# A gated decoder layer in split fp32 on one core: four plain gate-up jobs at the head of the feed-forward part, two half-width jobs in its middle

## The chip, the cores and the metric

The kernel runs on one core of a Trainium2 chip. TensorE (PE) multiplies matrices into PSUM; VectorE (DVE), ScalarE (ACT) and GpSimd (POOL) read and write SBUF and work beside it; SyncE (SP) issues most of the transfers. The metric is the device time of one execution in microseconds (us), the median of several.

## The reference

One layer of a decoder with 1024 channels, for 1024 prompt tokens and 8 sample tokens (1032 in all). The first part (attention, spatial gating, output projection, a residual) is not touched, except at its very end. The second part is what matters here:

```
h = _rmsnorm(x, g_fp)
f = (jax.nn.silu(h @ w_g) * (h @ w_u)) @ w_d
x = x + _rmsnorm(f, g_fq)
```

`w_g` and `w_u` are 1024 x 2816, `w_d` is 2816 x 1024.

## The kernel before

**Numbers.** Every fp32 operand of a product is held as two parts: a high part (ACT copies the operand into fp32r) and a low part (DVE subtracts the high part from the operand). A product is three matmuls: high by high, high by low, low by high.

**Shapes.** The 1032 tokens are four quarters of 258 columns (`NQ`); two quarters make a half (h = 0 or 1). The 2816 hidden channels are 22 tiles of 128 (`NF`). A *job* j multiplies one tile of `w_gate` and one of `w_up` by one half or by both. PE's order is the order of the program: the last units of the output projection (`wo_tile`, 24 units), then the 26 jobs, then the down projection `down(n, c)`, 16 times two.

**Blocks.** A job is seven *blocks* (`STEP`) for each half. A block is four steps in k times three matmuls, 12 matmuls of 128x258. With seven in place of eight, a job forms the 2 x 2 block product (Winograd's form of Strassen's method): it needs sums of the weight blocks (four per tile pair: POOL, `sums_in` three and `last_sum` one) and sums of the activation blocks (S1 to S4, four per half: three `f_sum` on POOL, one `f_third` on DVE), and it reads intermediate products back from PSUM (ACT copies one of them to `p1`; DVE makes seven sums and products in `ev`, `u2`, `u3`, C22, C21, prod1, C12, prod0, lines 2398 to 2456). Several blocks can start only when such a sum is there: the product is added up over the block's result in PSUM and SBUF in turn.

**Half jobs.** `HALVES` gives half 0 alone to jobs 0 to 3 (`AHEAD = 4`: half 1 isn't there yet), both halves to jobs 4 to 21, and half 1 alone to jobs 22 to 25, which load the weights of tiles 0 to 3 again. A job with both halves takes turns: a block of half 0, the same block of half 1. Each half has a set of three PSUM banks; in a job with one half the set is `j % 2`.

**Splits.** The weight blocks go through six slots (`SLOTS`). `high(q)` on ACT waits until the block six earlier has been used by PE, `low(q)` on DVE follows it (line 2324), and block q waits for `low(q)`. The activation blocks are split once: `f_high` on ACT (line 1687), `f_low` on DVE for A11, A12, S2, S1 (line 2318) and on POOL for S3, A22, S4 (line 2627). Their source is filled by `f_copy` (DVE) from PE's transposes (`f_turn`), the last three of which stand in job 2.

**Queues.** SP's queue is in program order: `job_load(j)` (1 MB of weights into one of two buffers, behind a wait for the splits of job j - 2), then `store(j - 2)`, which puts the result into HBM. At j = 23 twelve loads (`a_load(0)`, `a_load(1)`, the results of two quarters for the down projection) stand ahead of `store(21)` and `job_load(24)`. In `down` of n = 8, `z_first_sums` stands between the two halves and waits for POOL.

Of the kernel before, what the change touches and what calls it, by code (L numbers as in the profile page):

```python
# [12 lines left out]
ALU = mybir.AluOpType  # L13
# [66 lines left out]
F_HIGH = (0, 2, 1, 3, 4, 5, 6)  # L80
F_LOW = {0: (0, 1), 2: (0, 2), 1: (0, 3), 4: (0, 4), 3: (1, 1), 5: (1, 2), 6: (1, 3)}
# [4 lines left out]
DOWN = 7 * NJ  # L86
SPLITS = DOWN + 6 * 16
EVENTS = 7 * PAIRS
# [5 lines left out]
def tile_of(j):  # L94
    return j if j < NF else j - NF


def number(j, what, h, of):
    return len(of) * BEFORE[j] + of.index(what) * len(HALVES[j]) + HALVES[j].index(h) + 1


def event(j, o, h):
    return 7 * BEFORE[j] + o * len(HALVES[j]) + HALVES[j].index(h) + 1


def summed(j, what, h):
    return number(j, what, h, SUMS)


def silued(j, what, h):  # L110
    return number(j, what, h, SILUS)
# [7 lines left out]
def earlier(j, h):  # L119

    for i in range(j - 1, -1, -1):
        for g in reversed(HALVES[i]):
            if set_of(i, g) == set_of(j, h):
                return i, g
# [7 lines left out]
def used_after(q):  # L132

    if q < DOWN:
        return event(q // 7, q % 7, HALVES[q // 7][-1])
    return down_event((q - DOWN) // 6, 1, (q - DOWN) % 6)

# [42 lines left out]
def build(nc, A, O):  # L180
# [19 lines left out]
    with ctx:  # L200
# [105 lines left out]
        s0 = {i: at(f"s0_{i}", [P, 4, NQ], F32, R[3] + 4128 * i)[0] for i in (0, 1, 5)}  # L306
# [92 lines left out]
        f_tok, f_t, f_c, f_d = sem("f_scaled"), sem("f_turned"), sem("f_copied"), sem("f_s3_or_dec_done")  # L399
# [3 lines left out]
        sa_s, fh_s, fl_d, fl_p = sem("f_sums"), sem("f_hi"), sem("f_lo_dve"), sem("f_lo_pool")  # L403
# [4 lines left out]
        a_out, a_in = [sem(f"a_stored{i}") for i in range(2)], [sem(f"a_landed{i}") for i in range(6)]  # L408
        ah_s, al_s = sem("a_hi"), sem("a_lo")
# [23 lines left out]
        def f_raw(h, o):  # L433

            if STEP[o] in ("A11", "A12", "S3", "A22"):
                k = 4 * (STEP[o] in ("A12", "A22"))
                return fb[:, q_at(2 * h + (STEP[o] in ("S3", "A22"))), k:k + 4, :]
            return (s1 if h else s0)[{"S1": 0, "S2": 1, "S4": 5}[STEP[o]]][:, :, :]

        def f_lo(h, o):  # L440

            if STEP[o] in ("A11", "A12", "S3", "A22"):
                k = 4 * (STEP[o] in ("A12", "A22"))
                return fb_lo[:, q_at(2 * h + (STEP[o] in ("S3", "A22"))), k:k + 4, :]
            return (f1 if h else f0)[{"S1": 0, "S2": 1, "S4": 5}[STEP[o]]][:, :, :]

        def f_hi(h, o):
            return (f1 if h else f0)[{"A11": 2, "S2": 3, "A12": 4, "S3": 6, "S1": 7, "A22": 8, "S4": 9}[STEP[o]]][:, :, :]
# [29 lines left out]
        def split_source(q):  # L478
            if q < DOWN:
                w = w_pair(q // 7)  # L480
                return (w[:, 0, 0:4], tw[:, 1, :].rearrange("p (k c) -> p k c", k=4), w[:, 0, 4:8],
                        tw[:, 0, :].rearrange("p (k c) -> p k c", k=4), w[:, 1, 0:4], w[:, 0, 0:4], w[:, 1, 4:8])[q % 7]
# [40 lines left out]
        def _(sp):  # L523
# [92 lines left out]
            def job_load(j):  # L616

                if j >= 2:
                    sp.wait_ge(sp_lo, 7 * (j - 1))
                for e, w in enumerate((wg, wu)):  # L620
                    sp.dma_start(w_pair(j)[:, e], chunks(w, 0, 8, P * tile_of(j), P)).then_inc(raw_in[j % 2], 16)

            def store(j):
                hs = HALVES[j]
                cols = slice(2 * NQ * hs[0], 2 * NQ * hs[0] + 2 * NQ * len(hs))
                sp.wait_ge(sum_s, summed(j, "prod0", hs[-1]))
                sp.dma_start(a_d[tile_of(j)][:, cols], ab_of(j)[:, cols]).then_inc(a_out[j % 2], 16)

            def a_load(q):
                for kg, (k, n) in enumerate(KG):  # L630
# [2072 lines left out]
```

## Time and the profile before

| what | value |
|---|---|
| median of 3 runs | 1564.37 us (1560.65 to 1566.7) |
| the profiled execution's own time | 1565.85 us |
| its span in the trace | 1564.1 us |
| PE busy | 1491.3 us, 95% of the span |
| DVE, ACT, POOL busy | 757.0, 603.5, 270.0 us |
| mean granted TensorE clock | 0.981 |

The span is the trace from its first to its last instruction; the time has 1.75 us more around it. A matmul's busy time includes what the next one overlaps, so the spacing of matmuls is read from their starts, and PE's loss from its idle time and its granted clock (1.0 is 2.4 GHz).

### The profile page before, as it was taken

To read this page: it belongs to the slowest core of one execution; us is meant where nothing else is said; L and a number is where in the kernel's file an instruction comes from. 1 tells how busy PE (TensorE), PEld (TensorE's weight loads), DVE (VectorE), ACT (ScalarE), POOL (GpSimd) and SP (SyncE) were. 2 spreads that over 40 slices of the span, in tenths; PEclk is the share of its full clock that TensorE was granted. 3 is DMA by queue.
4 is the path that set the end of the run, shared out by engine and by line. 5 is a ranking of instruction groups with operands and counts; after the bars stand their busy time and mean duration, and the time that the engine had idled before them with its cause. 6 is when DMAs were issued, how large, how long until landed. Compare 5 with 4: busy or idle time off the path is not lost.

```text
span 1564.1 us, 26636 instructions
## 1 busy us (share of the span) xinstructions
PE 1491.3 (95%) x10953; PEld 1441.7 (92%) x10953; DVE 757.0 (48%) x1347; ACT 603.5 (39%) x1198; POOL 270.0 (17%) x253
## 2 busy tenths in 40 slices
PE   7999999999999999999876999999999689999998
PEld 6999999999999999987666999999999689999998
DVE  6105551343124464836789555666666473225322
ACT  6225543452224412446664333333333253335321
POOL 2000000000000132600545322222222120002000
PEclk9999999999999999999979999999999889999999
DMA  5111112001112153245532222222222746346341
GB/s 190 54 40 41 41 55 85 28 28 41 41 36 78 59 148 105 69 162 200 151 108 68 68 82 82 82 82 82 82 82 77 217 107 185 85 115 190 116 142 55
DMA packets 186665, 147.09 MB, mean 94 GB/s; under 512 B 7002, under 2 KB 168802, under 8 KB 186548
## 3 DMA queue, kind: packets, MB, share of 16 engines
q1 hardware_dynamic: 182656, 133.31, 28.3%
q0 software_dynamic: 2720, 7.89, 1.7%
q10 hardware_dynamic: 1172, 4.23, 0.7%
q8 instruction: 85, 1.39, 0.4%
q14 instruction: 32, 0.26, 0.1%
HBM read 121.84 MB, written 23.58 MB: 93 GB/s over the span
## 4 chain that ended last, share of the span: by engine, by line
PE 82%; DVE 6%; issue 3%; POOL 3%; ACT 2%; DMA 2%; SPq 1%; DVEq 0%; ACTq 0%; POOLq 0%
PE bank L734 8%; PE bank L736 8%; PE bank L735 8%; PE bank L1275 5%; PE bank L1276 5%; PE bank L1277 5%; PE psAB L1205 3%; PE bankC L734 3%; PE bank L1205 3%; PE bankC L736 3%; PE psAB L1207 3%; PE psAB L1206 3%; PE bankC L735 3%; PE bank L1206 3%; PE bank L1207 3%
## 5 line engine op out<-in xcount | busy, mean ns | idle before, releaser
L734 PE MATMUL bank<-h_hi,w_hi 128*128 128x344 f32 x752 | 247.9, 330 | 2.7 <-ACT g_pre L1345 2.2
L736 PE MATMUL bank<-h_hi,w_lo 128*128 128x344 f32 x752 | 240.1, 319 | 0.0
L735 PE MATMUL bank<-h_lo,w_hi 128*128 128x344 f32 x752 | 239.9, 319 | 0.0
L1275 PE MATMUL bank<-a_hi,s_hi 128*128 128x258 f32 x704 | 201.3, 286 | 0.0
L1276 PE MATMUL bank<-a_lo,s_hi 128*128 128x258 f32 x704 | 199.8, 284 | 0.0
L1277 PE MATMUL bank<-a_hi,s_lo 128*128 128x258 f32 x704 | 199.8, 284 | 0.0
L1884 DVE TENSOR_TENSOR w_lo<-w_raw,w_hi 128x1024 fp32r<-128x1024 f32 x71 | 90.8, 1279 | 202.0 <-ACT w_hi L1315 140.1
L1205 PE MATMUL psAB<-f,s_hi 128*128 128x258 f32 x440 | 128.9, 293 | 33.7 <-DVE ev L2411 13.9
L734 PEld LDWEIGHTS bank<-h_hi,w_hi 128*128 128x128 f32 x752 | 141.4, 188 | 7.4 <-issue 6.1
L735 PEld LDWEIGHTS bank<-h_lo,w_hi 128*128 128x128 f32 x752 | 141.3, 188 | 0.0
L736 PEld LDWEIGHTS bank<-h_hi,w_lo 128*128 128x128 f32 x752 | 141.3, 188 | 0.0
L1205 PE MATMUL bank<-f,s_hi 128*128 128x258 f32 x440 | 127.3, 289 | 11.3 <-ACT ev L1782 7.2
L1276 PEld LDWEIGHTS bank<-a_lo,s_hi 128*128 128x128 f32 x704 | 134.8, 191 | 0.0
L1275 PEld LDWEIGHTS bank<-a_hi,s_hi 128*128 128x128 f32 x704 | 134.2, 191 | 0.1
L1277 PEld LDWEIGHTS bank<-a_hi,s_lo 128*128 128x128 f32 x704 | 134.1, 190 | 0.0
L1708 ACT ACTIVATE s_hi<-raw 128x512 fp32r<-128x512 f32 x130 | 80.6, 627 | 127.5 <-PE psAB L1207 101.7
L1207 PE MATMUL psAB<-f,s_lo 128*128 128x258 f32 x440 | 127.1, 289 | 0.0
L1207 PE MATMUL bank<-f,s_lo 128*128 128x258 f32 x440 | 126.5, 287 | 0.0
L1205 PEld LDWEIGHTS psAB<-f,s_hi 128*128 128x128 f32 x440 | 86.2, 196 | 35.4 <-DVE ev L2411 14.1
L2324 DVE TENSOR_TENSOR s_lo<-rawd,s_hi 128x512 fp32r<-128x512 f32 x96 | 60.7, 646 | 115.1 <-ACT s_hi L1708 115.0
L2324 DVE TENSOR_TENSOR s_lo<-raw,s_hi 128x512 fp32r<-128x512 f32 x130 | 96.2, 771 | 21.7 <-ACT s_hi L1708 21.7
L1205 PE MATMUL bankC<-f,s_hi 128*128 128x258 f32 x352 | 100.4, 285 | 2.7 <-DVE ev L2424 2.0
(497 smaller groups left out, 3640.6 us busy)
## 6 DMA issues: line engine op xcount, KB each, us to landing
rawd<-in_w_down SPq DMA_DIRECT2D x32, 704.0 KB, 6.5
w_raw<-in_w_in SPq DMA_DIRECT2D x42, 512.0 KB, 4.0
raw<-in_w_gate SPq DMA_DIRECT2D x26, 512.0 KB, 4.0
raw<-in_w_up SPq DMA_DIRECT2D x26, 512.0 KB, 5.3
w_raw<-in_w_out SPq DMA_DIRECT2D x24, 512.0 KB, 3.7
a_raw<-a_rows SPq DMA_DIRECT2D x20, 516.0 KB, 7.3
a_rows<-ab SPq DMA_DIRECT2D x18, 516.0 KB, 2.7
xin<-in_x_prompt SPq DMA_DIRECT2D x8, 512.0 KB, 7.7
```

Source lines behind the costliest of these rows:

```text
L734: mm(out[:, 0:TG], w_hi[par][:, ws], hi[:, k, tgc[tg]], start=first, stop=False)
L735: mm(out[:, 0:TG], w_hi[par][:, ws], lo[:, k, tgc[tg]], start=False, stop=False)
L736: return mm(out[:, 0:TG], w_lo[par][:, ws], hi[:, k, tgc[tg]], start=False, stop=last)
L1205: mm(out, hi[:, k, :], xh[:, k, :], start=(begin and k == 0), stop=False, skip_group_check=True)
L1206: mm(out, hi[:, k, :], xl[:, k, :], start=False, stop=False, skip_group_check=True)
L1207: ins = mm(out, lo[:, k, :], xh[:, k, :], start=False, stop=(k == 3), skip_group_check=True)
L1275: mm(out, hi[:, k, :], xh[:, k, :], start=(kg == 0 and k == 0), stop=False)
L1276: mm(out, hi[:, k, :], xl[:, k, :], start=False, stop=False)
L1277: ins = mm(out, lo[:, k, :], xh[:, k, :], start=False, stop=(k0 + k == NF - 1))
L1708: fn(slot(q, 0), split_source(q), ACT.Copy).then_inc(sp_hi, 1)
L1884: v.tensor_tensor(w_lo[par][:], w_raw[par][:], w_hi[par][:].bitcast(F32), ALU.subtract).then_inc(w_lo_s, 1)
L2324: v.tensor_tensor(slot(q, 1), split_source(q), slot(q, 0).bitcast(F32), ALU.subtract).then_inc(sp_lo, 1)
```

## The change

Jobs 0 to 3 form all eight plain block products of half 0: `plain(j, o)` on PE has four weight blocks (B11, B21, B12, B22), each multiplied with two quarters. The gate product goes to banks 0 and 1 (c = 0, 1), the up product to banks 2 and 3 or 4 and 5. It is read back in two steps: ACT takes the gate bank through SiLU, DVE multiplies that with the up bank. No weight sums and no activation sums are needed for it. The sums of the activations (S1 to S4) and all low parts of activations move from POOL to DVE and stand later, in jobs 1 to 4; POOL makes the weight sums of jobs 4 to 25 alone. The half-1 jobs are now 9, 16, 24 and 25 (`ALONE`). The loads of the second quarter are spread: groups 2 to 5 follow the stores of their tiles, groups 0 and 1 and the first quarter come around job 25; `down_load(0)` comes earlier. `z_first_sums` stands three groups into `down(8, 1)`. The splits of the first quarter's results, two a job in jobs 23 to 25, now stand at the end of job 25 (two) and in `down(0)` (four). The diff, cut to its core:

```diff
+ALONE = (9, 16, 24, 25)
 NJ = NF + AHEAD
-HALVES = [(0,)] * AHEAD + [(0, 1)] * (NF - AHEAD) + [(1,)] * AHEAD
-BEFORE = [sum(len(x) for x in HALVES[:j]) for j in range(NJ + 1)]
-PAIRS = BEFORE[NJ]
+HALVES = [(0,) if j < AHEAD else (1,) if j in ALONE else (0, 1) for j in range(NJ)]
+TILE = [ALONE.index(j) if j in ALONE else j - sum(a < j for a in ALONE) for j in range(NJ)]
+PLAIN = ("B11", "B21", "B12", "B22")
...
+FIRST = [4 * min(j, AHEAD) + 7 * max(j - AHEAD, 0) for j in range(NJ + 1)]
+DOWN = FIRST[NJ]
...
+            done = [max(j for j in range(NJ) if 0 in HALVES[j] and TILE[j] < k + n) for k, n in KG]
+                if j > 12:
+                    for kg in range(2, 6):
+                        if done[kg] == j - 3:
+                            stored(j - 2)
+                            a_load(1, kg)
+                if j == NJ - 2:
+                    down_load(0)
+                if j == NJ - 1:
+                    stored(j - 2)
+                    sp.wait_ge(pe_ev, event(NJ - 3, 6, 0))
+                    for kg in range(5):
+                        a_load(0, kg)
+                    store(j - 2)
+                    a_load(1, 0)
+                    a_load(1, 1)
...
+            stored(NJ - 2)
+            for kg in range(6):
+                if done[kg] == NJ - 3:
+                    a_load(1, kg)
+            a_load(0, 5)
...
+            def plain(j, o):
+                q = FIRST[j] + o
+                pe.wait_ge(sp_lo, q + 1)
+                hi, lo = slot(q, 0), slot(q, 1)
+                for c in range(2):
+                    n = c if o < 2 else 2 + c + 2 * (j % 2)
+                    out = bank6[n][:, 0:NQ]
+                    if o == 0 and j == 0:
+                        pe.wait_ge(y_free[0], 7 + c)
+                    elif o == 0:
+                        pe.wait_ge(lu_s, 2 * j - 1 + c)
+                    elif o == 2 and j == 0:
+                        pe.wait_ge(y_free[0], 9)
+                        pe.wait_ge(y_free[1], 9)
+                    elif o == 2 and j >= 2:
+                        pe.wait_ge(sum_s, 2 * j - 3 + c)
+                    name = ("A11", "A21", "A12", "A22")[2 * (o % 2) + c]
+                    if j == 0 and o < 2:
+                        pe.wait_ge(fl_s, 2 * o + c + 1)
+                    xh, xl = f_hi(0, name), f_lo(0, name)
+                    for k in range(4):
+                        mm(out, hi[:, k, :], xh[:, k, :], start=(o % 2 == 0 and k == 0), stop=False, skip_group_check=True)
+                        mm(out, hi[:, k, :], xl[:, k, :], start=False, stop=False, skip_group_check=True)
+                        ins = mm(out, lo[:, k, :], xh[:, k, :], start=False, stop=(k == 3), skip_group_check=True)
+                    ins.then_inc(pe_ev, 1)
...
+                    if n == 8 and (c, kg) == (1, 3):
+                        z_first_sums()
...
+                for o in range(4 if j < AHEAD else 7):
+                    if j == 2 and o:
+                        f_turn(5 + o)
+                    if j < AHEAD:
+                        plain(j, o)
+                        continue
                     for h in HALVES[j]:
...
-                if n == 8:
-                    z_first_sums()
-                elif 9 <= n < 14:
+                if 9 <= n < 14:
...
-                    f_high(0, 0)
+                    f_high(0, "A11")
+                    f_high(0, "A21")
                     split_out(8 * g + 6)
                     y_first(g, 2)
-                    f_high(0, 2)
+                    f_high(0, "A12")
+                    f_high(0, "A22")
                     split_out(8 * g + 7)
-                    f_high(0, 1)
             high(0)
             high(1)
-            f_high(0, 3)
+            y_second(2, (0,))
             high(2)
-            f_high(0, 4)
-            y_second(2, (0, 1))
+            y_second(2, (1,))
             high(3)
-            f_high(0, 5)
             y_second(2, (2,))
-            f_high(0, 6)
             high(4)
...
+            def plain(j):
+                q = FIRST[j]
+                if j == 1:
+                    x1_squares()
+                elif j == AHEAD - 1:
+                    f_high(1, "A11")
+                    f_high(1, "A22")
+                high(q + 5)
+                if j == 0:
+                    y_root(2)
+                high(q + 6)
+                for c in range(2):
+                    act.wait_ge(pe_ev, plain_event(j, 1, c))
+                    if j >= 2:
+                        act.wait_ge(sum_s, 2 * j - 3 + c)
+                    fn(ev[:, 2 * (j % 2) + c, :], bank6[c][:, 0:NQ], ACT.Silu).then_inc(lu_s, 1)
+                if j == 1:
+                    f_scale(6)
+                high(q + 7)
+                if j == 1:
+                    f_scale(7)
+                    f_scale(8)
+                elif j == 2:
+                    for name in ("S2", "S3", "S1", "S4"):
+                        f_high(0, name)
+                elif j == AHEAD - 1:
+                    f_high(1, "S2")
+                    f_high(1, "A12")
+                    f_high(1, "S3")
+                high(q + 8)
+                if j == AHEAD - 1:
+                    f_high(1, "S1")
+                    f_high(1, "S4")
...
+                if j == NJ - 2:
+                    a_high(0, 0)
+                    a_high(0, 1)
+                elif j == NJ - 1:
+                    for kg in range(2, 6):
+                        a_high(0, kg)
...
+            def f_sum(h, name):
+                a11, a12, a21, a22, s2 = (f_raw(h, x) for x in ("A11", "A12", "A21", "A22", "S2"))
+                out = f_raw(h, name)
+                if h:
+                    dve.wait_ge(f_d, 1)
+                if name == "S1":
+                    ins = v.tensor_tensor(out, a21, a22, ALU.add)
+                elif name == "S2":
+                    dve.wait_ge(sa_s, 4 * h + 1)
+                    ins = v.tensor_tensor(out, f_raw(h, "S1"), a11, ALU.subtract)
+                elif name == "S3":
+                    dve.wait_ge(sa_s, 4 * h + 1)
+                    ins = v.tensor_tensor(out, a11, a21, ALU.subtract)
+                else:
+                    if h:
+                        dve.wait_ge(pe_ev, plain_event(AHEAD - 1, 2, 1))
+                    dve.wait_ge(sa_s, 4 * h + 2)
+                    ins = v.tensor_tensor(out, a12, s2, ALU.subtract)
+                ins.then_inc(sa_s, 1)
+            def f_low(h, name, n):
+                dve.wait_ge(fh_s, n)
+                if h or name[0] == "S":
+                    dve.wait_ge(sa_s, 4 * h + (3 if name == "A11" else 4))
+                v.tensor_tensor(f_lo(h, name), f_raw(h, name), f_hi(h, name).bitcast(F32), ALU.subtract).then_inc(fl_s, 1)
...
-                    f_third(0)
+                    f_low(0, "A11", 1)
+                    f_low(0, "A21", 2)
...
+            def plain(j):
+                q = FIRST[j]
+                low(q + 4)
+                if j == 0:
+                    y_var(2)
+                elif j == 1:
+                    f_sum(0, "S1")
+                    f_sum(0, "S2")
+                    dve.wait_ge(x1_sd, 7)
+                    v.reciprocal(stat[:, 21:24], stat[:, 18:21]).then_inc(x1_r, 1)
+                elif j == AHEAD - 1:
+                    f_sum(1, "S1")
+                    f_sum(1, "S2")
+                low(q + 5)
+                if j == 0:
+                    y_factor(2)
+                    x1_term(6)
+                    x1_add(6)
+                elif j == 1:
+                    f_sum(0, "S3")
+                    f_sum(0, "S4")
+                elif j == 2:
+                    f_copy(6)
+                elif j == AHEAD - 1:
+                    f_sum(1, "S3")
+                low(q + 6)
+                if j == 0:
+                    x1_term(7)
+                    x1_add(7)
+                    x1_term(8)
+                    x1_add(8)
+                elif j == 2:
+                    f_copy(7)
+                elif j == AHEAD - 1:
+                    f_low(1, "A11", 9)
+                low(q + 7)
+                if j == AHEAD - 1:
+                    f_sum(1, "S4")
+                for c in range(2):
+                    dve.wait_ge(lu_s, 2 * j + 1 + c)
+                    dve.wait_ge(pe_ev, plain_event(j, 3, c))
+                    if j >= 2:
+                        dve.wait_ge(a_out[j % 2], 16 * (j // 2))
+                    v.tensor_tensor(ab_of(j)[:, NQ * c:NQ * c + NQ], bank6[2 + c + 2 * (j % 2)][:, 0:NQ], ev[:, 2 * (j % 2) + c, :],
+                                    ALU.mult).then_inc(sum_s, 1)
+                if j == 2:
+                    f_copy(8)
+                    f_decode()
+                    for n, name in enumerate(("S2", "S3", "S1", "S4")):
+                        f_low(0, name, 5 + n)
+                elif j == AHEAD - 1:
+                    f_low(1, "S2", 11)
+                    f_low(1, "A12", 12)
+                    f_low(1, "S3", 13)
...
+                if j == NJ - 1:
+                    a_low(0, 0)
+                    a_low(0, 1)
...
+                if n == 0:
+                    for kg in range(2, 6):
+                        a_low(0, kg)
...
-            sums_in(0)
-            f_sum(0, 1)
-            f_sum(0, 2)
-            f_sum(0, 4)
-            f_low(0, 3)
-            last_sum(0)
-            f_low(0, 5)
-            f_low(0, 6)
-            for j in range(NJ):
-                if j + 1 < NJ:
-                    sums_in(j + 1)
-                if j == AHEAD - 1:
-                    f_sum(1, 2)
-                if j + 1 < NJ:
-                    last_sum(j + 1)
-                if j == 2:
-                    f_sum(1, 1)
-                if j == AHEAD - 1:
-                    f_sum(1, 4)
-                    for o in (3, 5, 6):
-                        f_low(1, o)
+            for j in range(AHEAD, NJ):
+                sums_in(j)
+                last_sum(j)
```

## Rows read from the trace of the kernel before

**Rows 1.** The page: PE's busy tenths in 40 slices.

```profile
PE   7999999999999999999876999999999689999998
```

**Rows 2.** Windows, by stage: busy us (instructions) by engine, granted clock, DMA.

```profile
1222.00:1238.00 16.00, 15.89 (x133) 15.68 (x131) 11.67 (x20) 6.20 (x12) 3.04 (x3) 1.00 0.74 242
774.00:850.00 76.00, 52.12 (x364) 50.01 (x363) 63.53 (x77) 41.75 (x71) 41.18 (x23) 0.87 0.31 89
850.00:879.00 29.00, 22.98 (x170) 22.59 (x170) 18.63 (x25) 10.86 (x20) 13.60 (x8) 0.88 0.16 47
879.00:1220.00 341.00, 341.00 (x2847) 341.00 (x2846) 207.84 (x358) 110.08 (x221) 91.61 (x69) 1.00 0.26 80
1220.00:1253.00 33.00, 18.99 (x155) 18.59 (x155) 15.15 (x25) 7.74 (x15) 7.32 (x6) 0.85 0.87 266
```

**Rows 3.** PE's waits from 700 to 1300 us: total, times, longest.

```profile
PE psAB L1205 <- DVE ev L2411: 13.9, 1, 13.9
PE psAB L1205 <- DVE ev L2398: 11.2, 3, 6.3
...
PE psAB L1205 <- issue: 4.6, 1, 4.6
```

**Rows 4.** PE's timeline: first matmuls of jobs 0, 5, 22 and of down.

```profile
773.95 0.28 PE L1205 MATMUL bank<-f,s_hi 128*128 128x258 f32 x1
...
878.64 0.28 PE L1205 MATMUL bank<-f,s_hi 128*128 128x258 f32 x1
...
1221.03 0.28 PE L1205 MATMUL bank<-f,s_hi 128*128 128x258 f32 x1
...
1285.27 0.28 PE L1275 MATMUL bank<-a_hi,s_hi 128*128 128x258 f32 x1
```

**Rows 5.** PE's timeline: unit 22 of the output projection, and a transpose.

```profile
764.28 0.50 PE L1152 MATMUL psAB<-w_hi,m_hi 128*128 128x512 f32 x1 [1.55 <-DVE w_lo L1884]
...
770.28 0.93 PE L730 MATMUL psT<-ident,t1a 128*128 128x128 f32 x7
```

**Rows 6.** DVE's timeline, 759 to 771 us.

```profile
759.64 1.23 DVE L2311 TENSOR_TENSOR fb<-fb 128x1032 f32<-128x1032 f32 x1 [2.32 <-POOL s L2616]
760.79 3.44 DVE L1884 TENSOR_TENSOR w_lo<-w_raw,w_hi 128x1024 fp32r<-128x1024 f32 x1
764.15 3.44 DVE L2318 TENSOR_TENSOR fb_lo<-fb,f 128x1032 fp32r<-128x1032 f32 x1
...
769.25 1.22 DVE L2318 TENSOR_TENSOR fb_lo<-fb,f 128x1032 fp32r<-128x1032 f32 x1
```

**Rows 7.** POOL's timeline, the same stretch.

```profile
759.68 3.46 POOL L2619 TENSOR_TENSOR s<-s,fb 128x1032 f32<-128x1032 f32 x1
```

**Rows 8.** Groups of DVE, 740 to 870 us: busy us, mean ns.

```profile
L2324 DVE TENSOR_TENSOR s_lo<-raw,s_hi 128x512 fp32r<-128x512 f32 x26 | 28.1, 1110 | 6.1 <-ACT s_hi L1708 6.1
```

**Rows 9.** Groups of DVE, 900 to 1200 us.

```profile
L2324 DVE TENSOR_TENSOR s_lo<-raw,s_hi 128x512 fp32r<-128x512 f32 x75 | 48.7, 682 | 0.0
L2456 DVE TENSOR_TENSOR ab<-ev 128x258 f32<-128x258 f32 x30 | 34.2, 1178 | 0.0
...
L2411 DVE TENSOR_TENSOR ev<-psAB,ev 128x258 f32<-128x258 f32 x15 | 6.4, 428 | 15.4 <-PE psAB L1207 15.4
```

**Rows 10.** ACT's timeline in the same stretch as rows 6.

```profile
757.48 1.07 ACT L1687 ACTIVATE f<-fb 128x1032 fp32r<-128x1032 f32 x1
```

**Rows 11.** Groups of POOL, 900 to 1200 us.

```profile
L2598 POOL TENSOR_TENSOR tw<-tw,raw 128x512 f32<-128x512 f32 x15 | 22.1, 1475 | 0.0
```

**Rows 12.** SP's queue, 1220 to 1255 us.

```profile
1226.84 13.70 SPq L631 DMA_DIRECT2D a_raw<-a_rows  x12
...
1241.34 2.87 SPq L621 DMA_DIRECT2D raw<-in_w_up  x1
```

**Rows 13.** PE's timeline at z_first_sums.

```profile
1422.45 0.35 PE L1217 MATMUL bankC<-one,acc 128*128 128x1 f32 x2 [2.39 <-POOL accd L2645]
```

**Rows 14.** DVE's timeline at the start of the down projection.

```profile
1286.34 1.83 DVE L2383 TENSOR_TENSOR a_lo<-a_raw,a_hi 128x1032 fp32r<-128x1032 f32 x2
```

More of the change, by code:

```diff
@@ L85, with before @@
 KG = [(4 * i, min(4, NF - 4 * i)) for i in range(6)]
-DOWN = 7 * NJ
+FIRST = [4 * min(j, AHEAD) + 7 * max(j - AHEAD, 0) for j in range(NJ + 1)]
+DOWN = FIRST[NJ]
 SPLITS = DOWN + 6 * 16
-EVENTS = 7 * PAIRS
+def before(j, plain, per_half):
+    return plain * min(j, AHEAD) + per_half * sum(len(HALVES[i]) for i in range(AHEAD, j))
+EVENTS = before(NJ, 8, 7)
+SUMMED = before(NJ, 2, 7)
 Z_ORDER = (0, 1, 2, 3, 8, 4, 5, 6, 7, 9)
@@ L91, with job_of, plain_event, t_sums @@
 Z_TURNED = {0: 2, 1: 3, 2: 4, 3: 5, 8: 6, 4: 8, 5: 9, 6: 10, 7: 10, 9: 11}
[L94 to L99, printed above, removed]
+def job_of(q):
+    return next(j for j in range(NJ) if q < FIRST[j + 1])
 def event(j, o, h):
-    return 7 * BEFORE[j] + o * len(HALVES[j]) + HALVES[j].index(h) + 1
+    return before(j, 8, 7) + o * len(HALVES[j]) + HALVES[j].index(h) + 1
+def plain_event(j, o, c):
+    return 8 * j + 2 * o + c + 1
 def summed(j, what, h):
-    return number(j, what, h, SUMS)
+    return before(j, 2, 7) + SUMS.index(what) * len(HALVES[j]) + HALVES[j].index(h) + 1
 def silued(j, what, h):
-    return number(j, what, h, SILUS)
+    return before(j, 2, 3) + SILUS.index(what) * len(HALVES[j]) + HALVES[j].index(h) + 1
+def t_sums(j):
+    return 4 * (j - AHEAD)
 def set_of(j, h):
@@ L119, in earlier @@
 def earlier(j, h):
-    for i in range(j - 1, -1, -1):
+    for i in range(j - 1, AHEAD - 1, -1):
         for g in reversed(HALVES[i]):
@@ L689, in _ @@
             store(NJ - 1)
-            for x in range(2):
-                sp.wait_ge(a_out[x], 8 * NJ)
+            stored(NJ)
             sp.wait_ge(pe_ev, EVENTS)
-            a_load(2)
+            for kg in range(6):
+                a_load(2, kg)
             for n in range(2, 16):
@@ L697, in _ @@
                     sp.wait_ge(pe_ev, down_event(7, 0, 5))
-                    a_load(3)
+                    for kg in range(6):
+                        a_load(3, kg)
                 if n == 10:
@@ L1844, in z_root @@
                 fn(stat[0:rows, n:n + 1], z_sum(t), ACT.Sqrt, scale=1.0 / D, bias=stat[0:rows, 62:63]).then_inc(z_sd, 1)
-            for j in range(NJ):
+            for j in range(AHEAD):
+                plain(j)
+            for j in range(AHEAD, NJ):
                 job(j)
@@ L2363, in _ @@
                 elif g == 2:
-                    f_low(0, 0)
+                    f_low(0, "A12", 3)
                 lo_out(8 * g + 7)
@@ L2481, in z_final @@
                                            ).then_inc(z_s, 1)
-            for j in range(NJ):
+            for j in range(AHEAD):
+                plain(j)
+            for j in range(AHEAD, NJ):
                 job(j)
```

287 lines of the change are left out of this document (109 added, 178 removed).

## The prediction

> **What bounds the kernel now.** I read the busy slices first: PE is at 9 tenths or more nearly everywhere, and two dips stand out, slices 20 to 22 and 32 to 33 [rows 1]. The windows put stages on them. From 879 to 1220 us PE is busy 341.00 of 341.00 us at full clock: the double jobs run at PE's own pace, and DVE (208 us), ACT and POOL are covered. From 774 to 850 us PE is busy 52 of 76 us at a clock of 0.87 while DVE is busy 63.5 us; from 1220 to 1253 it is busy 19 of 33 us [rows 2]. PE's waits name the causes: 11.2 us for the DVE sums of the half jobs, 4.6 us in job 4, and one wait of 13.9 us near the end, put down to DVE [rows 3]. SP's queue shows what that one is: the twelve loads of results hold the queue 13.7 us, and the weights of job 24 are issued only at 1241.34 [rows 12].
>
> Now the stages by PE's starts [rows 4]. The head (jobs 0 to 4) takes 878.64 - 773.95 = 104.7 us, the 17 double jobs 5 to 21 take 342.4 us, the end (jobs 22 to 25) 64.2 us. A double job is 342.4 / 17 = 20.14 us, so a block (a fourteenth) is 1.439 us and a half job 10.07 us. PE's own work in the head is 4 x 10.07 + 20.14 and three groups of transposes at 0.79 us (770.28 to the next start, 771.07) [rows 5]: 62.8 us, so 41.9 us are lost. In the end it is 40.3 us, and 24.0 are lost. The change can win at most these 65.9 us, less the work that it adds.
>
> **Added PE work.** Four jobs have eight blocks instead of seven: 4 x 1.439 = 5.8 us, certain, since PE is what bounds. The counts of double and half jobs stay 18 and 4.
>
> **The head, walked engine by engine.** I take each instruction in its engine's order at the duration of its row. On DVE: a weight split 0.60 to 0.68 us [rows 9], an activation split or sum (128x1032) 1.22 alone, but 3.44 beside POOL [rows 6, 7]; a product with a PSUM operand 0.43 [rows 9]. On ACT: an activation high part 1.07 [rows 10], SiLU from PSUM at most that of a copy of this size, under 0.5. The trace has no `f_sum` on DVE; the nearest is `f_third` of the same shape, 1.23 [rows 6].
>
> Unit 22 of the output projection waits 1.55 us for its low part, since the split took 3.44 us beside POOL [rows 5 to 7]. POOL is silent there now. ACT takes A11's high part at 757.48 [rows 10] and A21's behind it, to 758.5 and 759.5, DVE has both lows by 760.8 and the unit's own by 762.0; PE comes to it at 764.28 - 1.55 = 762.7. The wait goes, and the projection ends near 772.2: 1.8 us won (bounds: 0 and 1.8).
>
> Jobs 0 to 3 on PE are then 4 x 8 x 1.439 = 46.0 us plus transposes 2.4. Are they fed? Gate banks are read during the four up blocks (5.8 us), where ACT owes two splits, SiLU of two banks and a table load: hidden. The up banks alternate by job, so their product has a whole job. DVE's heaviest queue: in job 0 the residual of three token tiles (about 11 us) ends near 785.5, and the weight split behind it is due at 789.4; job 1 has four sums (4.9 us), four splits (2.6) and the two products, 8.4 of 11.5 us; job 2 has three copies, four splits, and behind its products the third copy and four lows of S1 to S4, done near 816. They are due at 821, when job 4 begins. Each is hidden. If this cover went, it would cost what is late in full. Weights: two buffers, and the load of job j + 2 leaves with the last of four splits, a whole job (11.5 us) ahead; fine as long as landing takes less than about 9 us.
>
> Job 3 is where the slack ends. DVE owes, for half 1, the sums S1 to S4 and the lows of A11, S2, A12, S3 beside four splits and two products: 8 x 1.2 + 4 x 0.65 + 0.9 = 13 us from 816, so to 829. PE wants S2's low at 825.5 and has it at 827.5; then `u2` of job 4 comes only at 833 behind S3's low and two weight splits, where PE wants it at 831.8. Together I find 3.6 us of waits in job 4 (now 4.6 and more, [rows 3]). POOL makes its eight weight sums for jobs 4 and 5 in that stretch, of about 1.35 to 1.48 us [rows 11]. Beside POOL a weight split is 1110 ns in place of 682 on the mean [rows 8, 9]; at that ratio some eight DVE operations lose 0.5 us each: 4 us more (bounds: 0, all hidden, and 8 x 1.4 = 11, each waiting out one POOL operation).
>
> The Trainium skill ("SBUF — State Buffer", section "Who interferes with whom") says that a DVE instruction with two SBUF inputs and a GpSimd one that reads SBUF exclude each other for the whole instruction. The rows fit it: 1.22 against 3.44 us, and 1178 ns for the product of two SBUF operands against 428 with one in PSUM [rows 6, 9]. By the rule alone I would take the upper bound, and the sum would be 7 us more.
>
> Head after: 46.0 + 2.4 + 20.1 + 3.6 + 4 = 76.1 us against 104.7, and 1.8 before it: 30.4 us won. The clock is won with it, since the pauses in front of the 0.87 and 0.88 windows are gone.
>
> **Half jobs 9, 16, 24, 25.** Do chains of one half stall without the DVE load of the head? Jobs 22 and 23 answer: PE is busy 15.9 of 16.0 us there, at full clock, with DVE at 11.7 [rows 2]. I charge 0.4 us each, 1.5 in all (bounds: 0 and 4 x 1.5, one late sum each).
>
> **The end.** Weights of job 25 now leave before the first loads of results; what is left beside them (five groups of the first quarter, two of the second) has 20 us. So the 13.9 us and the slow clock behind them go. Moved the other way: two lows of the first quarter now stand behind job 25's last product. Now that product ends and a low follows at 1286.34, when down has long begun [rows 14, 4]. Down has to wait for 1286.34 + 1.2 - 1285.27 = 2.3 us. The next four lows (1.2 each, a group of PE's is 1.43) just keep ahead; their highs on ACT (1.06) too.
>
> End and middle after: 17 x 20.14 + 4 x 10.07 + 1.5 + 2.3 = 386.5 against 342.4 + 64.2 = 406.6: 20.1 us won. **z_first_sums** stands 4 us later; its wait for POOL of 2.39 us [rows 13] is covered: 2.4 won (bounds: 0 and 2.4).
>
> **Sum.** 30.4 + 20.1 + 2.4 = 52.9 us. The profiled execution took 1565.85 us; 1513.0 is left. The median of the runs is 1.5 lower than that execution, so 1512, 3.4% less. Own range: 1503 with the charged waits at nothing (4 + 3.6 + 1.5); at the other ends POOL costs 7 more, the half jobs 4.5, unit 22 1.8 and z 2.4, and I take the first whole and a third of the rest: 1522.
>
> **Rivals.**
> *DVE bounds the head.* It gets seven lows and six sums more. For: DVE is busy 63.5 of 76 us now [rows 2]. Against: it loses 12 weight splits and 20 sums, and POOL's company. If its 23 sums and lows (1.22) cost 0.6 more each (half way to the 1110/682 ratio and beyond) and the slack is used up, 14 us: 1526. The Trainium skill's exclusion rule, named above, would by itself give 1519, between the forecast and this.
> *The end keeps its stall.* Loads still bunch round job 25, with two 0.7 MB loads of down weights. One wait like today's comes back: 13.9 us [rows 3], 1526. Against: the order of the queue.
> *Half jobs run as they do in the head now*, (104.7 - 20.1 - 4.6) / 4 = 20 us instead of 10.07: four times 9.9, so 1552. Against: jobs 22 and 23.
> *Slower: weights come too late.* The two buffers were built for jobs of 20.14 us; jobs of 11.5 and 10.07 us may outrun load, POOL's three sums (4.4 us) and split. If each of the seven jobs that follow or are a short one (0 to 3, after 9, 16, 24) stalls s, the gain is gone at s = 53 / 7 = 7.6 us and slower by 0.5% from 8.7; with today's 13.9 it is 1512 + 97 = 1609. For: the 13.9 us wait is of this kind. Against: the load leaves a job ahead, and job 23 followed 22 without a wait.
>
> **How the numbers follow.** Forecast 0.62, DVE 0.18, end stall 0.08, half jobs 0.05, weights 0.04; 0.03 for a mixture that comes out within half a per cent. Half a per cent (8 us) is about what this kernel's measurement tells from no change. Faster 0.93, same 0.03, slower 0.04. The range 1502 to 1532 takes in the first three with margin; it leaves 0.12 out, and a tail of the first.
>
> **What would show it.** PE's starts: job 4 at 821, job 5 at 847 (861 if DVE bounds), down 386 us after job 5; full clock from 774 on; no wait over 3 us for `s_lo` fed by a late `raw`. `f_low` on DVE at 1.2 us through job 2 and longer only from job 3. One wait of about 2.3 us at the first matmul of down. Wrong would be: weight splits waiting for `raw` in jobs 1 to 3, or DVE without idle time from 772 to 850.

## The result, and the profile after

| | before | after |
|---|---|---|
| median | 1564.24 us (4 runs, 1560.65 to 1566.7) | 1509.18 us (4 runs, 1506.99 to 1510.78) |
| profiled execution, its span | 1565.85, 1564.1 us | 1510.78, 1508.7 us |

The ratio is 0.9649, with a 95% interval of 0.9626 to 0.9671: 3.5% less, or 55 us. The forecast was 1512.

The page's two rows for TensorE, in 40 slices of the shorter span, answer to [rows 1]:

```profile
PE   7999999999999999999999999999999999999998
...
PEclk9999999999999999999999999999999999999999
```

The two dips are gone and the granted clock is 9 tenths or more in every slice. PE's waits from 700 to 1300 us, where [rows 3] had 13.9, 11.2 and 4.6 us:

```profile
PE bank L1357 <- DVE a_lo L2500: 2.3, 1, 2.3
PE bank L1285 <- DVE ev L2571: 1.4, 1, 1.4
...
PE bankC L1285 <- issue: 1.1, 1, 1.1
PE psAB L1285 <- issue: 0.9, 1, 0.9
```

PE's timeline at the first matmuls of job 0, job 4, job 5 and of down, beside [rows 4]:

```profile
772.81 0.28 PE L1252 MATMUL bank<-f,s_hi 128*128 128x258 f32 x1
...
821.72 0.28 PE L1285 MATMUL bank<-f,s_hi 128*128 128x258 f32 x1
...
846.06 0.28 PE L1285 MATMUL bank<-f,s_hi 128*128 128x258 f32 x1
...
1233.36 0.37 PE L1357 MATMUL bank<-a_hi,s_hi 128*128 128x258 f32 x1 [2.29 <-DVE a_lo L2500]
```

The head (jobs 0 to 4) is 846.06 - 772.81 = 73.3 us against 104.7; jobs 5 to 25 are 387.3 against 342.4 + 64.2 = 406.6; what follows the first matmul of down is 1508.7 - 1233.36 = 275.3 against 278.8; what comes before job 0 is 1.1 us shorter. These four are the whole difference of the spans, 55.4 us: 31.4, 19.3, 3.5 and 1.1, each rounded.

The clock is not full everywhere in the last stage. Behind the wait of 2.29 us the first matmuls of down start 0.22 us apart and not 0.12, until 1237 us: the half level (1.2 GHz). The window is of the changed kernel; the second is of a variant with the same wait (all half jobs at the end, below), whose clock stays full:

```profile
1235.00:1240.00 5.00, 5.00 (x37) 5.00 (x36) 5.00 (x7) 5.00 (x6) 0.00 (x0) 0.80 0.93 282
...
1235.00:1240.00 5.00, 5.00 (x42) 4.83 (x41) 4.88 (x6) 5.00 (x8) 0.00 (x0) 1.00 0.61 194
```

The first 100 matmuls of down take 13.6 us in the changed kernel and 12.0 in the kernel before, which has no wait there. So the 3.5 us of this stage are a balance: 5.1 won behind those 100 matmuls, at z_first_sums, and 1.6 lost in them.

The windows of jobs 0, 1, 2, 3 and 4 (busy us by engine: PE, PE's weight loads, DVE, ACT, POOL; then granted clock, DMA share, GB/s):

```profile
772.80:784.40 11.60, 11.60 (x98) 11.59 (x97) 9.75 (x15) 8.97 (x18) 0.00 (x0) 1.00 0.35 101
784.40:796.00 11.60, 11.60 (x99) 11.60 (x98) 9.57 (x14) 9.87 (x14) 0.00 (x0) 1.00 0.75 247
796.00:810.10 14.10, 14.10 (x121) 14.10 (x121) 5.96 (x10) 6.90 (x10) 4.17 (x3) 1.00 0.38 97
810.10:821.70 11.60, 11.60 (x98) 11.60 (x97) 11.16 (x14) 4.96 (x8) 2.15 (x1) 1.00 0.41 115
821.70:846.00 24.30, 20.89 (x170) 20.33 (x169) 23.84 (x30) 10.93 (x19) 9.23 (x6) 1.00 0.19 55
```

PE is busy all of the time through job 3, at full clock. DVE's idle time is not spread evenly: 1.9, 2.0, 8.1, 0.4 and 0.5 us in the five jobs. DVE's timeline, two rows in the output projection, one in job 3 (the sum S2 of half 1), two in job 4 (the low of S2, then those of A12 and S3):

```profile
759.90 2.38 DVE L2436 TENSOR_TENSOR f<-fb,f 128x1032 fp32r<-128x1032 f32 x2 [2.21 <-ACT f L1770]
762.20 1.22 DVE L1988 TENSOR_TENSOR w_lo<-w_raw,w_hi 128x1024 fp32r<-128x1024 f32 x1
...
818.73 2.13 DVE L2420 TENSOR_TENSOR s<-s,fb 128x1032 f32<-128x1032 f32 x1
...
826.69 1.66 DVE L2436 TENSOR_TENSOR f<-s,f 128x1032 fp32r<-128x1032 f32 x1
828.28 4.55 DVE L2436 TENSOR_TENSOR fb_lo<-fb,f 128x1032 fp32r<-128x1032 f32 x2
```

The lows of A11 and A21 take 2.38 us for both and unit 22's own 1.22, where [rows 6] had 3.44 each. The last three rows take 2.13, 1.66 and 4.55 us where 1.22 an operation, 4.9 in all, would be alone: POOL makes its weight sums for jobs 4 and 5 beside them (817.6 to 819.8 and 825.1 to 831.7 us). Job 4 takes 24.3 us, against 20.2 of the double jobs behind it; its three waits are 1.13 us at 824.45, 0.88 at 828.45 and 1.40 at 834.43. The first two are named `issue` in the list of waits, but each ends 0.1 us behind a low (A11's at 824.35, S2's at 828.35).

### The profile page after: what moved, and what is told of

The parts are those of the page before. It is cut to its first block, busy times and chain, and to the rows that moved or that the text cites. A ratio compares the mean times of both kernels' runs of the same rounds, so it can differ in the third digit from the quotient of the medians.

```text
span 1508.7 us, 26632 instructions
## 1 busy us (share of the span) xinstructions
PE 1484.0 (98%) x11001; PEld 1437.7 (95%) x11001; DVE 732.6 (49%) x1328; ACT 595.7 (39%) x1183; POOL 214.5 (14%) x225
## 4 chain that ended last, share of the span: by engine, by line
PE 92%; DVE 4%; ACT 1%; DMA 1%; issue 1%; DVEq 0%; ACTq 0%
PE bank L787 9%; PE bank L789 9%; PE bank L788 9%; PE bank L1357 6%; PE bank L1358 6%; PE bank L1359 6%; PE bankC L787 3%; PE bankC L789 3%; PE bankC L788 3%; PE psAB L1285 3%; PE bank L1285 3%; PE psAB L1287 3%; PE psAB L1286 3%; PE bank L1286 3%; PE bank L1287 3%; PE psT L783 3%
## 5 line engine op out<-in xcount | busy, mean ns | idle before, releaser
L1988 DVE TENSOR_TENSOR w_lo<-w_raw,w_hi 128x1024 fp32r<-128x1024 f32 x71 | 87.6, 1234 | 204.8 <-ACT w_hi L1398 142.9
L1285 PE MATMUL psAB<-f,s_hi 128*128 128x258 f32 x400 | 113.5, 284 | 1.0 <-issue 0.9
L1287 PE MATMUL psAB<-f,s_lo 128*128 128x258 f32 x400 | 112.7, 282 | 0.0
L1285 PE MATMUL bank<-f,s_hi 128*128 128x258 f32 x328 | 92.9, 283 | 1.6 <-DVE ev L2571 1.4
L1287 PE MATMUL bank<-f,s_lo 128*128 128x258 f32 x328 | 92.6, 282 | 0.0
L2442 DVE TENSOR_TENSOR s_lo<-raw,s_hi 128x512 fp32r<-128x512 f32 x126 | 86.8, 717 | 3.4 <-ACT s_hi L1794 3.4
L1286 PE MATMUL bank<-f,s_hi 128*128 128x258 f32 x296 | 83.6, 282 | 0.0
L787 PE MATMUL bankC<-h_hi,w_hi 128*128 128x344 f32 x256 | 82.9, 324 | 0.0
```

Of the source, the lines that this page charges most:

```text
L787: mm(out[:, 0:TG], w_hi[par][:, ws], hi[:, k, tgc[tg]], start=first, stop=False)
L1285: mm(out, hi[:, k, :], xh[:, k, :], start=(begin and k == 0), stop=False, skip_group_check=True)
L1286: mm(out, hi[:, k, :], xl[:, k, :], start=False, stop=False, skip_group_check=True)
L1287: ins = mm(out, lo[:, k, :], xh[:, k, :], start=False, stop=(k == 3), skip_group_check=True)
L1988: v.tensor_tensor(w_lo[par][:], w_raw[par][:], w_hi[par][:].bitcast(F32), ALU.subtract).then_inc(w_lo_s, 1)
L2442: v.tensor_tensor(slot(q, 1), split_source(q), slot(q, 0).bitcast(F32), ALU.subtract).then_inc(sp_lo, 1)
```

## The experiments

For each, the span of PE's work from job 0 to down (460.6 us in the changed kernel, 511.3 in the kernel before) is the closest measure, since the start of job 0 moves by up to 2.3 us from one execution to the next (770.5 to 772.8 in the changed kernel and its variants). A second run of the changed kernel gave 460.6 again, and a median of 1508.52 us, ratio 0.9644.

### The end: order of the loads, or place of the half jobs

**The changed kernel, weights of job 25 issued late.**

```diff
-                job_load(j)
+                if j < NJ - 1:
+                    job_load(j)
...
                     a_load(1, 1)
+                    job_load(j)
```

> The changed kernel, with one order undone: the weights of job 25 are issued behind the seven loads of results and the store. If the order of SP's queue is what won the end (my theory), PE waits 7 to 13 us at job 25 and the time is 1516 to 1522 us, against 1509. If the place of the half jobs won it, the time stays within 2 us of 1509.

It took 1525.54 us, ratio to the kernel before 0.9746 [0.973, 0.9762]: 16 us more than the changed kernel, and 3.5 more than the upper end of what I expected. PE's wait, and SP's queue:

```profile
PE bank L1287 <- DVE ev L2583: 12.8, 1, 12.8
```

```profile
1212.64 1.67 SPq L663 DMA_DIRECT2D a_raw<-a_rows  x2
1214.35 1.29 SPq L653 DMA_DIRECT2D raw<-in_w_gate  x1
1215.68 4.16 SPq L653 DMA_DIRECT2D raw<-in_w_up  x1
```

The weights leave at 1214.35 to 1215.68, and at 1197.14 in the changed kernel. The wait of 12.8 us stands in job 24 (1208.28 to 1235.46), behind its fifth block, and not in job 25, whose weights are late. ACT's and DVE's timelines show why:

```profile
1226.26 0.63 ACT L1796 ACTIVATE s_hi<-raw 128x512 fp32r<-128x512 f32 x1 [15.42 <-DMA raw<-in_w_up]
```

```profile
1226.92 1.14 DVE L2444 TENSOR_TENSOR s_lo<-raw,s_hi 128x512 fp32r<-128x512 f32 x1 [14.47 <-ACT s_hi L1796]
1227.98 0.41 DVE L2583 TENSOR_TENSOR ev<-bank,ev 128x258 f32<-128x258 f32 x1
```

DVE's sum `u3` of job 24, for which PE waits, needs nothing of job 25, but in DVE's order it stands behind a split of job 25's weights, and that waits for ACT and for the landing. The 13.9 us in the kernel before are the same chain: they stand behind the fifth block of job 23, for the weights of job 24. Order alone brings the stall back. From job 0 to down it costs 17.7 us (478.3 against 460.6): this wait, one of 1.3 us behind it, and the granted clock, which is 0.50 from 1228.4 to 1236 us.

**The kernel before, result loads behind the weights of job 24.** (The second quarter's loads got a semaphore of their own.)

```diff
-                if j == NF + 1:
+                if j == NF + 2:
                     sp.wait_ge(pe_ev, event(NF - 1, 6, 0))
...
                     a_load(0)
                     a_load(1)
```

> The kernel before, with one order changed: the twelve loads of results are issued behind the weights of job 24 and no longer ahead of them. My theory: the wait of 13.9 us and the slow clock behind it mostly go, a shorter wait at job 25 stays (its weights are still behind the loads); 1546 to 1553 us. If the place of the half jobs won the end, the wait only moves one job on and the time stays at 1562 to 1566.

1556.99 us, ratio 0.9949 [0.9932, 0.9966]: 8 us won, less than I said. (In the kernel before, the twelve loads stand behind `store(21)`, and ahead of `job_load(24)` and `store(22)`.) The wait of 13.9 us in job 23 is gone and one comes in job 24, since the weights of job 25 still stand behind the twelve loads:

```profile
PE bank L1206 <- DVE ev L2415: 9.3, 1, 9.3
```

**The same, behind the weights of job 25 too** (`j == NF + 3`).

> The kernel before with the result loads behind the weights of job 24 and of job 25 (the run before this one moved only job 24's and PE waited 9.3 us at job 25 instead). If the order of the queue is all that the end lost, jobs 22 to 25 take 42 to 46 us instead of 64.2 and the time is 1544 to 1549 us. If the load of weights is too slow for half jobs in a row in the kernel before, a wait of over 5 us stays at job 24 or 25 and the time is above 1552.

1550.74 us, ratio 0.9905 [0.988, 0.993]; job 5 to down is 391.4 us, 15.3 less than before. The time lies between the two that I had named, and neither reason is the one: no job waits for weights any more, but ACT waits in its own order for the first loaded results, and PE behind it (ACT's timeline, then PE's):

```profile
1247.74 1.06 ACT L1722 ACTIVATE a_hi<-a_raw 128x1032 fp32r<-128x1032 f32 x1 [3.84 <-DMA a_raw<-a_rows]
```

```profile
1251.67 0.58 PE L1206 MATMUL bank<-f,s_hi 128*128 128x258 f32 x1 [4.38 <-ACT ev L1786]
```

So 15.3 of the 19.3 us of the stage come from keeping weights ahead of results. What is left is near the 4.4 us of this wait. The changed kernel doesn't have it; it has loaded three groups of the second quarter earlier and asks for the results one job later, but no run took these two alone.

**The changed kernel, all half jobs at the end.**

```diff
-ALONE = (9, 16, 24, 25)
+ALONE = (22, 23, 24, 25)
...
-                    sp.wait_ge(pe_ev, event(NJ - 3, 6, 0))
+                    sp.wait_ge(pe_ev, event(NF - 1, 6, 0))
```

> The changed kernel with all four half jobs at the end (22 to 25) as before, the order of the loads kept as the change has it. My theory, that a half job costs no more at one place than at another: within 2.5 us of 1509. Rival, that spreading them matters since four loads of 1 MB fall into 40 us beside the loads of results: 1518 to 1525, with waits for late weights at jobs 24 and 25.

1509.67 us, ratio 0.9642 [0.9626, 0.9658], beside 0.9649 and 0.9644 for the changed kernel: the place of the half jobs can't be told in the time. The trace has 1.8 us more from job 0 to down, in two waits for DVE's sums where half jobs follow one another; behind down's first matmul it is 1.3 us shorter than the changed kernel, by the clock (above):

```profile
1208.42 0.39 PE L1285 MATMUL psAB<-f,s_hi 128*128 128x258 f32 x1 [0.52 <-DVE ev L2589]
...
1215.92 0.39 PE L1285 MATMUL bank<-f,s_hi 128*128 128x258 f32 x1 [1.48 <-DVE ev L2571]
```

### The head: plain products, POOL's silence, or DVE

**The kernel before, POOL's activation sums and lows made by DVE.** The six `f_sum` and six `f_low` of POOL stand at DVE's nearest places; jobs 0 to 3 keep seven blocks and their read-backs, and POOL the weight sums.

```diff
@@ POOL
-            f_sum(0, 1)
-            f_sum(0, 2)
-            f_sum(0, 4)
-            f_low(0, 3)
...
@@ DVE
+                    f_sum(0, 1)
+                    f_sum(0, 2)
                     f_third(0)
+                    f_sum(0, 4)
...
             low(2)
+            f_low_p(0, 3)
             f_low(0, 4)
             low(3)
+            f_low_p(0, 5)
+            f_low_p(0, 6)
```

> The kernel before with one part of the change alone: POOL's six sums and six low parts of activations are made by DVE; the head keeps its seven-block jobs and their read-backs. My theory, that the head is long because each block waits for a read-back behind a full DVE queue: 12 more operations of 1.2 us against some 11 us less of POOL's company, so 1560 to 1572 us. Rival, that POOL's company made the head slow and the plain products matter little: 1540 to 1550.

1554.86 us, ratio 0.9936 [0.9919, 0.9952]: 10 us faster, where I had said none. It is more work for DVE and yet a gain. The head took 868.15 - 770.60 = 97.6 us against 104.7, and job 0 began 3.4 us earlier. But the long waits for the read-backs are there still:

```profile
PE psAB L1205 <- DVE ev L2428: 11.6, 3, 6.3
PE bank L1205 <- ACT ev L1782: 7.2, 1, 7.2
```

The first is 11.6 us, in [rows 3] 11.2. The second, the first read-back of job 0 behind ACT's activation splits, was 7.2 us in the kernel before too. So of the 31.4 us of the head, 7.1 come with the move alone, and 24.3 need the rest of the change, whose core there is the plain products. By PE's starts (us; job 2 has the transposes):

| job | before | POOL's work on DVE | changed kernel |
|---|---|---|---|
| 0 | 22.8 | 21.3 | 11.6 |
| 1 | 19.8 | 19.9 | 11.6 |
| 2 | 13.9 | 13.9 | 14.2 |
| 3 | 19.2 | 17.6 | 11.6 |
| 4 | 29.0 | 24.9 | 24.3 |

The move won its time in jobs 0, 3 and 4; the rest won its in jobs 0, 1 and 3, and nothing in job 2. The result lies between my two expectations, so neither holds alone.

**The changed kernel with POOL's company back.** Sixteen additions of 128x512 on POOL, into a buffer that nobody reads then: four from 767 us on, ahead of job 0, and twelve in jobs 0 to 2.

```diff
+            for i in range(16):
+                pool.wait_ge(sp_lo, i // 4 * 4 + 1)
+                g_.tensor_tensor(tw[:, 1, :], tw[:, 0, :], tw[:, 0, :], ALU.add).then_inc(dum, 1)
```

> The changed kernel with 16 additions of 128x512 on POOL during jobs 0 to 3 (four a job, like the weight sums that the change removed; results unused). My theory: DVE's operations on two SBUF operands get longer, but DVE is idle 13 of 48 us there, so PE loses 0 to 4 us: 1509 to 1513. Rival, that POOL's silence is what lets the head run at PE's pace: 10 us more or above, 1519 to 1529.

1509.69 us, ratio 0.9648 [0.9626, 0.9669]: no difference. The company was felt, though. The window of jobs 0 to 3, and the group of DVE's weight splits with it and, below, without:

```profile
772.00:820.00 48.00, 47.85 (x397) 47.58 (x396) 42.29 (x51) 30.53 (x49) 25.21 (x17) 1.00 0.48 143
```

```profile
L2443 DVE TENSOR_TENSOR s_lo<-raw,s_hi 128x512 fp32r<-128x512 f32 x15 | 13.8, 932 | 1.8 <-ACT s_hi L1795 1.8
```

```profile
L2442 DVE TENSOR_TENSOR s_lo<-raw,s_hi 128x512 fp32r<-128x512 f32 x15 | 10.2, 692 | 2.4 <-ACT s_hi L1794 2.4
```

A split took 932 ns instead of 692 and DVE was busy 42.3 us instead of 34.9 (the same window of the changed kernel), and PE lost 0.3 us in job 2 and nothing else. Small POOL operations cost next to nothing where DVE has room. What the move won in the run above would then be the long ones, which stood beside operations that PE was waiting for [rows 6, 7]; that follows from the two runs together and was not tested by itself.

**The changed kernel with DVE's work doubled.** The 16 weight splits and S1, S2, S4 of half 0 are each made twice.

```diff
+                if 4 <= q < 20:
+                    st.link(v.tensor_tensor(slot(q, 1), split_source(q), slot(q, 0).bitcast(F32), ALU.subtract))
                 v.tensor_tensor(slot(q, 1), split_source(q), slot(q, 0).bitcast(F32), ALU.subtract).then_inc(sp_lo, 1)
```

> The changed kernel with the 16 weight splits of DVE in jobs 0 to 3 and three activation sums made twice, about 14 us more of DVE work. My theory: jobs 0 to 2 absorb theirs, job 3 hands on some 2.5 us to job 4: 1511 to 1516. Rival, that DVE bounds the head: all 14 us show, 1522 to 1525.

1518.36 us, ratio 0.9712 [0.9691, 0.9732]: 9 us more, between the two. The windows of job 1 and of the time after it, and PE's longest wait:

```profile
783.00:794.30 11.30, 11.30 (x96) 11.30 (x95) 11.09 (x16) 7.10 (x12) 0.00 (x0) 1.00 0.42 118
794.30:805.00 10.70, 6.83 (x58) 6.62 (x56) 10.49 (x16) 9.31 (x14) 0.00 (x0) 1.00 0.50 173
```

```profile
PE psT L783 <- DVE fb L2395: 5.1, 1, 5.1
```

Job 1 had 2.0 us to spare and was given some 6 us, so DVE is 10.5 of 10.7 us busy in job 2 and reaches the copy of a transposed tile late; PE waits 5.1 us for it in front of the next transpose, although DVE had 8 us idle in job 2 of the changed kernel. Job 2 becomes 7.8 us longer by it, and job 4 2.9. My 13 us of slack were right as a sum over the head and wrong as cover: it is what each job has left that counts.

### The terms at the seams

**z_first_sums back between the halves of down 8** (one run, with the profile).

```diff
-                    if n == 8 and (c, kg) == (1, 3):
-                        z_first_sums()
...
+                if n == 8:
+                    z_first_sums()
```

> The changed kernel with z_first_sums back between the two halves of the ninth down step. My theory: PE waits 2.4 us there again and the span is 1511.1 us instead of 1508.7. Rival, that the later place only moves the wait: 1508.7, no wait there.

The span was 1510.9 us. What follows down's first matmul took 278.9 us against 275.3, so in this run the place costs 3.6 us, not 2.4. PE's timeline (the wait, and two matmuls after it) has both parts:

```profile
1370.72 0.35 PE L1297 MATMUL bankC<-one,acc 128*128 128x1 f32 x2 [2.38 <-POOL accd L2776]
...
1373.49 0.42 PE L1355 MATMUL bank<-a_hi,s_hi 128*128 128x258 f32 x1
1373.71 0.42 PE L1356 MATMUL bank<-a_lo,s_hi 128*128 128x258 f32 x1
```

The wait is 2.38 us. Behind it come the nine short products of the sums (2 us), and then the matmuls of down start 0.22 us apart until 1376, where they start 0.12 apart at the full clock: the half level (1.2 GHz) came with the pause. The rest of the 3.6 us, 1.2, goes there. In the profile before the same place cost 5.1 us (above), since the half level lasted until 5.8 us behind the sums, and here until 3.4.

**Two lows of the first quarter moved into job 25.**

```diff
+                if j == NJ - 1:
+                    a_low(0, 0)
+                    a_low(0, 1)
                 low(q + 6)
```

> The changed kernel with the first two low parts of the first quarter's results moved in DVE's order from behind job 25's last product to behind its first sum. My theory: the wait of 2.3 us at the first matmul of down goes and nothing else grows, 1506.9 against 1509.2. Rival: the two operations of 1.2 us make job 25's own read-backs late and the 2.3 us reappear there.

1508.61 us, ratio 0.9643 [0.9623, 0.9663], no difference from the changed kernel. The wait at down's first matmul is gone and job 25 is not longer by it (10.6 us), and 5.5 us behind down's first matmul comes another wait (PE, and ACT):

```profile
1234.53 0.55 PE L1357 MATMUL bank<-a_hi,s_hi 128*128 128x258 f32 x1 [2.52 <-DVE a_lo L2500]
```

```profile
1228.52 3.48 ACT L1807 ACTIVATE a_hi<-a_raw 128x1032 fp32r<-128x1032 f32 x4
```

The third low waits for its high part, and ACT makes four of those only behind the last SiLU of job 25. Neither theory had it: the wait moved to the next operand of the same kind.

**A version with both repaired.** Four lows and the highs of groups 2 and 3 go into job 25; in job 2 the lows of S2 and S3 and the third copy go ahead of the products, into DVE's 8 idle us.

```diff
+                if j == 2:
+                    f_low(0, "S2", 5)
+                    f_copy(8)
+                    f_decode()
+                    f_low(0, "S3", 6)
...
+                if j == NJ - 1:
+                    a_low(0, 2)
+                    a_low(0, 3)
...
+                if j == NJ - 1:
+                    a_high(0, 2)
+                    a_high(0, 3)
```

> The changed kernel with three moves. Two low parts of S2 and S3, and the third copy, go ahead of job 2's products on DVE (their high parts earlier on ACT), into time in which DVE is idle; the first four low parts of the first quarter's results go into job 25 (before only two had gone and PE waited at the third group). My theory: the 3.4 us of waits in job 4 and the 2.3 us at down go, 1503 to 1506 us. Rival, that DVE is full from job 3 on and the waits only shift: 1507 to 1511.

1503.65 us (1503.14 to 1504.93), ratio 0.9613 [0.9596, 0.9631], beside 0.9644 [0.9626, 0.9662] for the changed kernel on the same chip. The medians are 4.9 us apart and the runs don't overlap (the changed kernel's lowest is 1507.49). PE's waits left in jobs and down, and a window over job 4 (821.1 to 842.1 us) and the first of job 5:

```profile
PE psAB L1285 <- DVE ev L2604: 1.5, 1, 1.5
PE bank L1285 <- DVE ev L2580: 0.5, 1, 0.5
```

```profile
822.00:846.00 24.00, 23.50 (x195) 23.29 (x195) 23.54 (x32) 9.20 (x18) 11.07 (x7) 1.00 0.19 57
```

Job 4's waits went from 3.4 to 0.5 us, and the job from 24.3 to 21.0. DVE is busy there 23.5 of 24 us still. The work moved into job 2 (two lows and a copy of two operations) is near 4 us, and DVE's queue in job 3 and 4 runs that much ahead, so a full DVE and results that stand too late in its order are one and the same here; the run doesn't part them. The other repair moved its wait rather than took it: the 2.3 us at down are gone, and 1.5 us for DVE's sum, new, stand in job 25, so that job 5 to down is 387.1 us against 387.3. Its gain is behind that: without the pause the clock stays full at the start of down, and what follows its first matmul takes 273.8 us against 275.2.

## Why the prediction was right

By its own steps:

- *Added PE work, 5.8 us*: jobs 0 to 3 take 821.72 - 772.81 = 48.9 us, forecast 46.0 + 2.4 = 48.4. PE is the bound there, as said.
- *The projection's end*: 1.8 us said, 1.1 between the two profiles; the wait of 1.55 is down to 0.36. The start of job 0 moves by more than this from one execution to the next, so the 1.1 alone shows little.
- *Job 4's waits and POOL's company in it*: 3.6 + 4 us charged, 24.34 - 20.14 = 4.2 measured, of which 1.13 + 0.88 + 1.40 = 3.4 are waits: at the low of A11, which the walk didn't name, at that of S2 and at `u2`, which it did. This is the mis-sized term of the head (76.1 said, 73.3 measured). That the waits alone come near the 3.6 is luck: the company is inside them. Beside POOL, DVE's four operations ahead of `u2` took 3.5 us more than 1.22 each (2.13, 1.66 and 4.55 us), and from job 3 on DVE was never idle for long. By my estimate, with these 3.5 us taken out of DVE's queue, the lows of A11 and S2 would be late by 0.2 and 0.5 us and `u2` not at all. So what was too large is the walk's own 3.6: it had DVE through with S3's low at 829, and two splits and the operation of `u2` (0.4) bring that to 830.7, not to the 833 that it took. No run took POOL's sums out of job 4, so the split of the 4.2 us stays an estimate.
- *The upper bound for the company*: by the exclusion rule of the Trainium skill ("SBUF — State Buffer", "Who interferes with whom") I would have charged 7 us more. The durations bear the rule out here too (932 against 692 ns); the time doesn't follow from it, since a longer DVE operation is not yet a wait of PE.
- *Middle and end*: 386.5 said, 387.3 measured, since the double jobs take 20.19 us and not 20.14; a half job takes 10.45, 0.4 more than 10.07, as charged; the wait at down 2.3 said and 2.29 measured. The reason, the order of the queue, is shown for 15.3 us of it. That the half jobs cost little wherever they stand is shown too. The row that the prediction rests this on ends at 1238.0, 0.6 us ahead of the 13.9 us, which stand in job 23 itself; that the wait was the queue's and not the half jobs' the experiments show, not this row.
- *z_first_sums*: 2.4 said as the bound, 3.5 measured for the stage, and that is 5.1 won at this place less 1.6 lost at the start of down. Two terms are missing, of opposite sign: the half clock behind the old pause, and the half clock behind the new one of 2.3 us. "Full clock from 774 on" is not met for the 3.4 us from 1233.6 on.

The errors are small and of both signs (2.8 us too careful in the head, 1.1 in the stage of z, 0.7 too bold before job 0 and 0.8 in middle and end), and the sum was 2.2 us short: 52.9 against 55.1 by the profiled executions. That they cancel in part is luck. Of the rivals, DVE as the bound of the head is refuted for jobs 0 to 3 of the changed kernel, and the doubling shows how near it was: 2 us a job in jobs 0 and 1. In job 4, where DVE is busy 23.8 of 24.3 us, it does hold PE up, by the 4.2 us. The stall at the end comes back only when the order is undone, half jobs don't run as in the old head, and no job waits for weights.

Several of my expectations on the experiments were worse than the prediction. The two on the order of the queue missed their ranges by 3.5 and 4 us: the slow clock behind a wait, and the wait that remains, cost more than I gave them. I took POOL's and DVE's exchange as even for the kernel before, by adding up durations; it won 10 us. And I took slack as one sum.

What stays open: of the 24.3 us of the head that need the rest of the change, the table gives 9.8 to job 0, 8.3 to job 1 and 6.0 to job 3, but how much in each is a read-back and how much a late sum no run took apart.

## What to carry to other kernels

A chain of short blocks with a read-back between them can cost more than the work that it saves: eight plain products of which nothing is awaited beat seven with seven sums, where the other engines are full. Ask of slack not how much there is in a stage but what stands in the queue in front of the instruction that is awaited. A wait named for an engine's sum can be one for what stands ahead of it there, here the split of the next job's late weights. Keep the loads that feed the next job ahead of bulk loads in a shared queue, and when you move one operand forward, look which one is late next.

## What the runs showed of the hardware

- A pause of PE of 2.3 to 2.4 us was followed by matmuls 0.22 us apart instead of 0.12 in some executions and not in others. Behind 2.38 us and nine short products it cost 1.2 us more than the pause, and 2.7 in the kernel before, whose granted clock from 1420 to 1430 us was 0.69 on the mean. Behind 2.29 us at the start of down, the first 100 matmuls took 13.6 us in four executions (the changed kernel twice, with POOL's company and with z_first_sums back) and 12.3 in three others with the same wait; 12.0 without a wait. With the nine short products and no pause ahead of them (1373.9 to 1375.7 us), the next matmuls of the changed kernel start 0.12 us apart.
- In SP's queue twelve loads of results, issued back to back, held the issue of what follows for 13.7 us in the kernel before [rows 12], and for 16.8 us in the run with the weights ahead of them.
- DVE's splits of 128x512 took 932 ns on the mean beside POOL's additions of 1478 ns, 692 without; splits and lows of 1.22 us took up to 3.44 beside POOL's sums of 3.46.
